# Down projections of a two-layer encoder: seven quadrant products for eight, K in three groups

## The reference

```python
def conv_gated_ffn(h, w_up, conv_w, conv_b, w_down):
    a = h @ w_up                                  # 1024 -> 5632
    a = lax.conv_general_dilated(a, ...) + conv_b # depthwise, width 3, along the tokens
    gate, val = jnp.split(a, 2, axis=-1)
    return (jax.nn.silu(gate) * val) @ w_down     # 2816 -> 1024
...
x = x + conv_gated_ffn(rmsnorm(x, ffn_norm_g[i]), ffn_w_up[i], ...)
```

## Time and profile before

| | us |
|---|---|
| median of 3 runs | 2043.03 (2042.94 to 2043.03) |
| profiled execution, its own time | 2045.53 |
| its span, first to last instruction | 2043.7 |
| PE busy | 2008.1 (98%) |
| DVE busy | 1245.5 (61%) |
| ACT busy | 943.2 (46%) |
| POOL busy | 337.0 (16%) |
| down projection of layer 0, on PE | 841.8 to 1081.2 |
| down projection of layer 1, on PE | 1801.0 to 2040.4 |
| granted TensorE clock, mean | 0.996 |

### The profile page before, as it was taken

One profiled execution on the slowest core, in us unless ns is written; L12 is line 12 of the kernel. 1 busy time (PEld: TensorE's weight loads), 2 busy tenths in 40 slices (PEclk: granted clock), 3 DMA queues, 4 the chain that ended last, 5 costly groups with the idle time before them and its releaser, 6 DMA issues.

```text
span 2043.7 us, 24674 instructions
## 1 busy us (share of the span) xinstructions
PE 2008.1 (98%) x9316; PEld 1657.5 (81%) x9316; DVE 1245.5 (61%) x1687; ACT 943.2 (46%) x1445; POOL 337.0 (16%) x238
## 2 busy tenths in 40 slices
PE   8999899998999999999999999999999999999999
PEld 8988567887888888888888888788788888888887
DVE  5288785588776777634536344549877776753433
ACT  6233687645555554423434532334555555542231
POOL 0022100352223223000102000125223223200000
PEclk9999999999999999999999999999999999999999
DMA  5111000412532232444443211141252332244444
GB/s 173 31 42 31 28 17 9 146 52 71 167 93 75 81 93 73 144 142 152 139 165 107 79 41 32 52 144 51 73 175 68 87 93 74 78 160 145 148 140 175
DMA packets 193646, 196.50 MB, mean 96 GB/s; under 512 B 32768, under 2 KB 147968, under 8 KB 193536
## 3 DMA queue, kind: packets, MB, share of 16 engines
q1 hardware_dynamic: 193392, 194.81, 30.7%
q10 hardware_dynamic: 144, 0.21, 0.0%
HBM read 159.33 MB, written 35.65 MB: 95 GB/s over the span
## 4 chain that ended last, share of the span: by engine, by line
PE 82%; issue 12%; DVE 3%; ACT 2%; POOL 0%; POOLq 0%; ACTq 0%; DVEq 0%
PE bank L790 21%; PE bank L791 21%; PE bank L792 21%; PE bank L546 4%; PE bank L547 4%; PE bank L548 4%; PE bank L648 1%; PE bank L649 1%; PE bank L650 1%; PE bank L731 1%; PE bank L712 1%; DVE bl L1451 1%; PE bank L699 1%; PE bank L928 1%; ACT pT L1095 0%
## 5 line engine op out<-in xcount | busy, mean ns | idle before, releaser
L790 PE MATMUL bank<-bh,spl 128*128 128x512 f32 x1064 | 416.2, 391 | 10.7 <-ACT rstd L1200 5.7
L792 PE MATMUL bank<-bh,spl 128*128 128x512 f32 x1064 | 415.2, 390 | 0.0
L791 PE MATMUL bank<-bl,spl 128*128 128x512 f32 x1064 | 415.0, 390 | 0.0
L790 PE MATMUL bank<-hid_h,down_h 128*128 128x512 f32 x704 | 273.9, 389 | 0.0
L791 PE MATMUL bank<-hid_l,down_h 128*128 128x512 f32 x704 | 273.9, 389 | 0.0
L792 PE MATMUL bank<-hid_h,down_l 128*128 128x512 f32 x704 | 273.9, 389 | 0.0
L1451 DVE TENSOR_TENSOR hid_l<-hid_w,hid_h 128x1024 fp32r<-128x1024 f32 x88 | 107.8, 1225 | 269.6 <-ACT hid_h L1334 269.6
L790 PEld LDWEIGHTS bank<-bh,spl 128*128 128x128 f32 x1064 | 200.6, 188 | 55.2 <-ACT rstd L1200 6.6
L792 PEld LDWEIGHTS bank<-bh,spl 128*128 128x128 f32 x1064 | 200.4, 188 | 42.0
L791 PEld LDWEIGHTS bank<-bl,spl 128*128 128x128 f32 x1064 | 200.6, 189 | 41.2
L1334 ACT ACTIVATE hid_h<-hid_w 128x1024 fp32r<-128x1024 f32 x88 | 93.2, 1060 | 297.9 <-DMA down_w<-w_down 297.9
(11 more groups left out here) (217 smaller groups left out, 3767.5 us busy)
## 6 DMA issues: line engine op xcount, KB each, us to landing
raw<-w_up SPq DMA_DIRECT2D x88, 512.0 KB, 5.4
hid_w<-hidden_kept SPq DMA_DIRECT2D x88, 512.0 KB, 3.4
hidden_kept<-hidden SPq DMA_DIRECT2D x88, 256.0 KB, 2.3
down_w<-w_down SPq DMA_DIRECT2D x88, 256.0 KB, 3.8
x_kept<-x SPq DMA_DIRECT2D x16, 512.0 KB, 6.5
x<-x_kept SPq DMA_DIRECT2D x16, 512.0 KB, 8.7
gws<-w_in SPq DMA_DIRECT2D x32, 256.0 KB, 3.2
qws<-w_qkv SPq DMA_DIRECT2D x24, 256.0 KB, 3.8
```

Source lines behind the costliest of these rows:

```text
L790: mm(out, wh, ah, start=first, stop=False, skip_group_check=True)
L791: mm(out, wh, al, start=False, stop=False, skip_group_check=True)
L792: return mm(out, wl, ah, start=False, stop=last, skip_group_check=True)
```

## The change

Each down projection becomes six pairs of jobs `t` = 0 to 5. K (22 tiles) is cut into three groups of 6, 8 and 8 tiles, each in two halves of `HALF` = 3, 4, 4 tiles. For a group there are two pairs, one for each half of the output columns; a pair is two jobs `i`, a job two output tiles. Each job is seven products, each of 3 or 4 tiles of K (9 or 12 matmuls), in the order P1, P2, P6, P5, P7, P3, P4, each for i = 0 and i = 1.

- PE: 7·(2·6 + 4·8)·3 = 924 matmuls per layer for 1056; 1848 for 2112 in both (`down_product`).
- Input quadrants: seven per group, each split by ACT (`part_hi`) and DVE (`part_lo`), 128x1536 or 128x2048. P6, P5, P7 and P4 are sums. DVE makes one (`t3`), POOL five additions per group (`part_sum`: T2A, T1, T2B, T4A, T4B). T2B needs a third transfer into a buffer that T2A has read (`third_term`).
- Weight quadrants: POOL makes eight sums per pair (`down_sum`), ACT and DVE split 14 per pair (`hi_down`, `w_lo`), now through the ring `spl`, 128x384 or 128x512.
- Results: since K is in three groups, all of `x` is added to in each. Per pair ACT copies six banks out (`copy`), POOL adds the six copies to `x` (`add_copy`), and DVE adds eight banks (`evict`). Before, there were 16 evictions per layer and no copies.
- Transfers per layer: of `hidden_kept` 12 quadrants per group, 33 MiB in rows of 2 KB, for 22 MiB in rows of 4 KB; of `w_down` the same 11 MiB, now in rows of 512 B, one buffer per job (`raw_load_down`), free for the next pair when the low part of P4's weight is made.
- At the seam to the gMLP the buffers of its first weights are numbered anew (`slab_slot`), its inputs are made in the new order of `GROUPS`.

The core of the diff:

```diff
+HALF = (3, 4, 4)
+FIRST = (0, 6, 14)
+NPAIR = 2 * len(HALF)
+DORDER = tuple((t, o, i) for t in range(NPAIR) for o in range(NOP) for i in range(2))
...
+            def down_product(layer, t, o, i):
...
+                if o == P6:
+                    pe.wait_ge(d_cp, 6 * pair + 1 + i)
...
+                if o == P4:
+                    pe.wait_ge(x_add, x0 + 3 + i)
+                if t % 2 == 0 and i == 0:
+                    pe.wait_ge(d_lo, NOP * (pair // 2) + SPLIT.index(o) + 1)
+                pe.wait_ge(sp_lo, layer * NENT + n + 1)
...
+                for k in range(h):
+                    last = triple(out, w[:, 0, k], w[:, 1, k], part["hi"][o][:, k], part["lo"][o][:, k],
...
+            def third_term(layer, g):
+
+                sp.wait_ge(d_sum, 5 * (layer * len(HALF) + g) + T2A)
+                quadrant(layer, g, 0, 0, ffn_mem[layer]["down"][HALF[g]]["first"][P6], P6)
...
+                for t in range(NPAIR):
+                    g = t // 2
+                    if t % 2 == 0:
+                        if t:
+                            part_load(layer, g, P1)
+                        part_load(layer, g, P2)
+                        part_load(layer, g, P6)
+                    if t == 0:
+                        raw_load_down(layer, t, 1)
+                    if t % 2 == 0:
+                        part_load(layer, g, P5)
+                    if t:
+                        raw_load_down(layer, t, 0)
+                        raw_load_down(layer, t, 1)
+                    if t % 2 == 0:
+                        part_load(layer, g, P7)
+                        third_term(layer, g)
...
+                for t in range(NPAIR):
+                    begins, g = t % 2 == 0, t // 2
+                    add_copy(t, 0)
+                    add_copy(t, 1)
+                    if begins:
+                        part_sum(g, T4A)
+                    for i in range(2):
+                        down_sum(t, S3, i)
+                    for i in range(2):
+                        down_sum(t, S4, i)
+                    if begins:
+                        part_sum(g, T4B)
+                    for c in range(2, 6):
+                        add_copy(t, c)
+                    if not begins and t < NPAIR - 1:
+                        for step in (T2A, T1, T2B):
+                            part_sum(g + 1, step)
+                    if t < NPAIR - 1:
+                        first_sums(t + 1)
```

More of the change, by code:

```diff
@@ new lines, in quadrant, with part_load @@
+            def quadrant(layer, g, half, s, dst, o):
+                k0 = FIRST[g] + half * HALF[g]
+                sp.wait_ge(h_st[s], 16 * (layer * NUP + k0 + HALF[g]))
+                sp.dma_start(dst[:], hidden[layer, k0:k0 + HALF[g], :, s].rearrange("k p n -> p k n")) \
+                    .then_inc(d_ld[o], 16)
+            def part_load(layer, g, o):
+                m = ffn_mem[layer]["down"][HALF[g]]
+                part_free(sp, layer, 2 * g, o)
+                whole = {P1: (0, 0), P2: (1, 0), P6: (1, 1), P5: (0, 1), P7: (1, 1), P3: (1, 1), P4: (1, 0)}[o]
+                quadrant(layer, g, *whole, m["whole"][o], o)
+                if o in (P6, P7):
+                    quadrant(layer, g, 0, 1, m["first"][o], o)
+                if o in (P5, P4):
+                    quadrant(layer, g, 0, 0, m["first"][o], o)
@@ new lines, in up_job, with part_hi @@
+                    mid(j, 1)
+                    hi(n0 + 9)
+                    mid(j, 2)
+                def part_hi(g, o):
+                    gi = layer * len(HALF) + g
+                    m = mem["down"][HALF[g]]
+                    if o in (P1, P2, P3):
+                        act.wait_ge(d_ld[o], 16 * (gi + 1))
+                    elif o == P7:
+                        act.wait_ge(d_t3, gi + 1)
+                    else:
+                        act.wait_ge(d_sum, 5 * gi + {P6: T2B, P5: T1, P4: T4B}[o])
+                    part_free(act, layer, 2 * g, o)
+                    A(m["hi"][o][:], m["whole"][o][:], ACT.Copy).then_inc(d_hi, 1)
@@ new lines, in copy @@
+                def copy(t, c):
+                    o, i = (P1, P6, P5)[c // 2], c % 2
+                    number = (layer * NPAIR + t) * 6 + c
+                    act.wait_ge(prod, w0 + DPOS[t, o, i] + 1)
+                    if t == 0 and c < 2:
+                        act.wait_ge(c_add, adds_before(layer, NUP))
+                    if t == 0 and 2 <= c < 4:
+                        act.wait_ge(h_st[c - 2], 16 * (layer * NUP + NUP))
+                    if number >= 4:
+                        act.wait_ge(d_x, number - 3)
+                    b = 4 + i if o == P5 else (0, 6)[t % 2] + i
+                    A(mem["copies"][number % 4], bank[:, b], ACT.Copy).then_inc(d_cp, 1)
@@ L1835, in evict, with part_lo @@
[L1835 to L1841 removed]
+                def part_lo(g, o):
+                    gi = layer * len(HALF) + g
+                    m = mem["down"][HALF[g]]
+                    dve.wait_ge(d_hi, NOP * gi + SPLIT.index(o) + 1)
+                    if o == P7:
+                        dve.wait_ge(d_sum, 5 * gi + T4A)
+                    lo(m["lo"][o][:], m["whole"][o][:], m["hi"][o][:]).then_inc(d_lo, 1)
@@ new lines, in first_sums, with part_sum @@
+                def first_sums(t):
+                    for kind in (S1, S2):
+                        for i in range(2):
+                            down_sum(t, kind, i)
+                def part_sum(g, step):
+                    gi = layer * len(HALF) + g
+                    m = mem["down"][HALF[g]]
+                    o = {T2A: P6, T1: P5, T2B: P6, T4A: P4, T4B: P4}[step]
+                    a, b, op = m["whole"][o], m["first"][o], ALU.add if step == T2B else ALU.subtract
+                    if step == T4A:
+                        b = m["whole"][P7]
+                        pool.wait_ge(d_t3, gi + 1)
+                    if step == T2B:
+                        pool.wait_ge(d_ld[o], 48 * gi + 48)
+                        pool.wait_ge(d_sum, 5 * gi + T2A)
+                    elif step == T2A:
+                        pool.wait_ge(d_ld[o], 48 * gi + 32)
+                    else:
+                        pool.wait_ge(d_ld[o], 32 * gi + 32)
+                    if step == T4B:
+                        pool.wait_ge(d_sum, 5 * gi + T4A)
+                    G.tensor_tensor(a[:], a[:], b[:], op).then_inc(d_sum, 1)
```

436 lines of the change are left out of this document (285 added, 151 removed).

## The result

The changed kernel takes 2221.36 us (median of 4 runs, 2221.09 to 2222.26); the kernel before took 2042.99 beside it (2042.6 to 2043.03). The ratio is 1.0871, with a 95% interval of 1.0857 to 1.0886. The forecast was 2170 with a range of 2075 to 2225, and the sum worked out before the discount was 2177. So 178 us were added where the sum had 134. The order of events was the forecast one but for one place in each group; there, at the first group of each layer and at the seam the list was too short. The 2221 lie 1 us above the range of the likeliest case (2130 to 2220) and inside that of the clock (2195 to 2260, chance 0.08).

The account below looks back on a forecast made before the run. PE bounded the old kernel; after the change, DVE and POOL turns plus late transfers would. Two layers +130.8 and seam +3 on 2045.5 gave 2179, 2177 as run median, put at 2170; range 2075 to 2225.

Parts of the forecast that it names:

- the discount: Whole kernel: forecast put at 2170, 7 below the sum of 2177, because strict alternation is the costliest way to share.
- the list: Down projections: hand-made sequence of some forty turns per group, with times from T2B's end; a full group costs 108.6 us.
- the likeliest case: Down projections: DVE and POOL take turns and transfers come late, as followed; 2130 to 2220, chance 0.50.
- the clock: Rival, down projections: PE drops to 1.2 GHz after the longest stops, adding 33 us: 2210; range 2195 to 2260, chance 0.08.
- What the change takes off PE: Both down projections: 264 fewer matmuls at 0.2267 us each take off 59.8 us, which alone would give 1983.
- DVE and POOL do not add up side by side: Down projections: two-SBUF-input DVE operations and POOL's exclude each other; 90.9 us per full group, floor 244 per layer, +5.
- Where the order costs more than the floor: Down projections: order of turns and late loads gives groups of 105.6, 108.6 and 90.6 us: 304.8 per layer, +65.4.
- Transfers: Down projections: 370 GB/s for 2 KB rows; two 512 KB weight loads take 5.4 us; T2B's third term lands about 104.
- The seam: Seam to the gMLP: an eviction and a weight split now stand between two matmuls, some 2 to 4 us, +3.
- Turns alone, no transfer late: Rival, down projections: engines take turns but loads arrive in time; 2055 to 2130, middle 2090, chance 0.33.
- No change: Rival, down projections: no turns, but late transfers cost 70 us in all: 2056; range 2039 to 2060, chance 0.03.
- Faster: Rival, down projections: little alternation and early loads, so PE bounds again: 2001, range 1983 to 2038, chance 0.06.

## Why the prediction was right, and where it was short

The mechanism was the forecast one, and the measured time lies in the range, 4 us from its end. The profiled executions differ by 177 us where the sum had 134. Of the 43 that it lacked, 34 lie in the two stages (22 of them in the first groups, 11 in the middle ones) and 9 outside them.

**What the change takes off PE.** Right in the count, 264 instructions fewer. The 60 us never showed, since PE's time is not what counts in most of the stage; leaving out a further 140 gave 51.

**DVE and POOL do not add up side by side.** Right, and the largest term: with POOL's operations cut 153 of 178 us go, and in the kernel before they can be made with 24 idle subtractions. Pitches, not durations: by the list of 0.60, 2.20, 1.20 and 4.57 the trace was followed within 1.7 us over forty turns.

**Where the order costs more than the floor.** The first two thirds of the list were right. The failed place is the end of the odd pair. The step was "T2A holds the engines 80.1 to 84.7 and T1 85.3 to 89.9", with the loads issued at 90.5 for P4's second weight. I gave DVE one turn between T2A and T1 and spent it on the weight's part; in the trace P2's large low part came first, and so each of the two DVE operations waited for a whole large sum. P4's parts were done at 91.9 and 93.1 and not at 85.3 and 90.5. The second was 2.6 us late. Because both came together, the queue then held 1.05 MB of weights more than the list had there, by the estimate above the other 3.1 us. Together that is the 5.6 us of a middle group.

**Transfers.** The weights of the odd pair took 7.2 us and not 5.4 (issued at 44.1, landed at 51.3 on the table's scale), which used up what the list had too much before them; over all of them the page has 6.4, against 5.4 in the earlier trace rows:

```profile
raw<-w_down SPq DMA_DIRECT2D x32, 512.0 KB, 6.4
```

The rate of 370 GB/s for 2 KB rows was good: three quadrants took 8.1 us for 8.5. Two steps of the list do not come out of its own terms. Its 3.2 + 5.7 + 2.8 from 90.5 end at 102.2, not at about 104, and its 19.4 us from 8.3 before the stage end at 11.1, not at 12.7; each has 1.6 to 1.8 us more with no row named. The trace had use for them: at the two starts T2B ended at 18.7 and 19.5 for 17.

**The first group.** It took 114.7 and 118.5 for 105.6 and was the largest miss. In layer 0 the start gave 1.7 us of it; the even pair ended at 59.8 and not 55.4, T1 at 92.0 and not 87.4, P4's second low part at 93.5 and not 88, and the third term landed 16.7 us after it and not 13. The middle groups were 114.2 and 113.7 for 108.6; the last, with nothing behind it, 90.8 and 92.1 for 90.6. PE's matmuls were at half speed from 845.19 to 875.76; how much of the even pair's 4 us that is, no run separates.

**The seam.** "+3" measured +14 between the two stages (719.8 to 733.6 us); the first stage began 2 us earlier than before, so some 12 in all. PE on its first matmuls of the gMLP in the changed kernel:

```profile
1161.62 0.47 PE L707 MATMUL bank<-gw,act2h 128*128 128x512 f32 x1 [2.05 <-issue]
...
1162.40 0.63 PE L707 MATMUL bank<-gw,act2h 128*128 128x512 f32 x1
```

Two us of eviction and split were in the forecast. A second wait of 5.5 us for `gw` at 1171.69, since DVE makes the gMLP's input late and the weights behind it, and half-speed matmuls (some 3 us) were not. The two stages grew by 80.4 and 84.9 us to PE's last product in them; with these 12 that is the 177 by which the span grew.

**The discount.** I took 7 us off because "a strict alternation is the costliest way to share". The trace alternates strictly. It was a guess with no row, and it was wrong.

**The rivals.** *Turns alone, no transfer late* (2055 to 2130) would be the kernel without third load; that one took 2176, so turns with the rest of the chain cost more than I gave them. *No change* fell, but its working was good: it is nearly the run with all of POOL cut, 2068.6 for 2056. *Faster* fell. *The clock* was put down as a rival with 33 us, and was there besides. PE at P6 of the second group, after its longest stop there, and where the odd pair of that group starts:

```profile
964.06 0.77 PE L849 MATMUL bank<-dhi,spl 128*128 128x512 f32 x1 [12.45 <-DVE spl L1595]
...
1007.66 0.47 PE L849 MATMUL bank<-dhi,spl 128*128 128x512 f32 x1 [2.36 <-DVE spl L1595]
...
1008.66 0.51 PE L850 MATMUL bank<-dlo,spl 128*128 128x512 f32 x1
1008.97 0.63 PE L851 MATMUL bank<-dhi,spl 128*128 128x512 f32 x1
1009.39 0.63 PE L849 MATMUL bank<-dhi,spl 128*128 128x512 f32 x1
```

The pitch at half speed is 0.43 us and not 0.23, which is 1.2 for 2.4 GHz. Of the 19 slow stretches in the two stages 16 are there from the first matmul after a stop, of 3.2 to 13.5 us, as at 964.06. In the other three the clock falls some 1 us after matmuls have begun again, as at 1008.97, and it is back at 1012.30, in the next product. The granted clock of both stages is 0.87. What the pitches of slow matmuls have above 0.2267 adds up to 24 us in layer 0 and 22 in layer 1. It is an estimate what of these 46 us is in the time: PE's work was worth 51/126 of itself, so some 19. The rest passes while DVE isn't ready anyway. No run changed the clock alone, so this stays open. The Trainium skill (TensorE: Matmul & The Clock Gate, section Part 1: The HAM clock gate (the "warmup" mystery)) has PE fall when idle and come back with work; the 16 stretches that are slow from their first matmul agree.

## What to carry to other kernels

Before work is given to an idle GpSimd, look at what DVE does there: each of its two-SBUF-input operations and each GpSimd operation that reads SBUF is paid by both engines, so add the two columns, not the larger of them, and compare with PE. Additions that can take one input from PSUM are free of it. A large sum is dearer on GpSimd (4.6 us) than on DVE (2.3), but moving it to DVE pays only where it does not stand ahead of something that PE waits for. A saving on PE should be checked against what feeds PE: here 60 us fewer matmuls came with 91 us of turns on DVE and GpSimd for each full group, which has 76 us of matmuls, and not even free input sums made it faster than before.

## What the hardware showed that was not expected

- A GpSimd operation of 128x2048 that nothing holds takes 4.53 us for a sum of two buffers (T2B) and 3.60 for a buffer with itself; filling one takes 1.81 us and holds nobody.
- The turns are one for one at every size seen: a DVE part of 0.68 us waits for the whole GpSimd operation of 3.6 to 4.6, once per operation, and GpSimd for it. So a short operation loses most: 0.68 became 4.08, and 1.23 became 4.02.
- TensorE was at 1.2 GHz from the first matmul after 16 stops of 3.2 to 13.5 us, and in three cases fell amid matmuls, about 1 us after they had begun again behind a stop of 2.4 to 3.4 us. It cost some 46 us of matmul time, three quarters of the 60 us that the change took off PE.
